# A two-layer hybrid encoder step: other layouts and another order for six small pieces of work

## The reference, cut to what matters

```
h = RMSNorm(x);  proj = h @ w_in        # columns go to four groups A, B, C, D of 256 channels
A: depthwise conv + RG-LRU scan         # lru_x, lru_g
B: latent attention: q from q_lat, k and v from 128-wide latents,
   new ones and 512 cached ones (past_ckv @ mla_wkv_b)
C: retention, 4 heads of 64             # r_q, r_k, r_v, r_g
D: mLSTM, 4 heads of 64                 # m_q, m_k, m_v, m_o, m_if
   dm = bh[t] - bh[s] + ig[s] (masked);  m_t = max(bh + m, max_s dm)
   sc = (q k^T) * exp(dm - m_t);  num = sc v + exp(bh + m - m_t) * (q C^T)
   state C <- gl * C + sum_s ws v k
x += concat(A, B, C, D, normed per head and gated) @ w_out
x += (silu(h2 @ w_g) * (h2 @ w_u)) @ w_down,   h2 = RMSNorm(x)
```

## Time and profile before

| | |
|---|---|
| median of three runs | 970.5 us (969.1 to 970.56) |
| the profiled execution | 969.53 us, of which the span of instructions is 967.7 us |
| TensorE busy | 951.0 us of the span, 98% |
| VectorE, ScalarE, GpSimd busy | 507.3, 200.7, 398.8 us |
| granted TensorE clock | 1.00 of full |
| HBM | 115 GB/s over the span |

### The profile page before, as it was taken

The page is one execution under the profiler, slowest core; times in us unless marked ns, Lnnn a source line. Parts: engine busy times, 40 slices in busy tenths (PEclk is TensorE's granted clock), DMA queues, the critical chain, the costliest instruction groups (busy, mean ns, idle before and its releaser), DMA issues. The chain is left out here.

```text
span 967.7 us, 15109 instructions
## 1 busy us (share of the span) xinstructions
PE 951.0 (98%) x5875; PEld 842.9 (87%) x5875; DVE 507.3 (52%) x1013; ACT 200.7 (21%) x440; POOL 398.8 (41%) x386
## 2 busy tenths in 40 slices
PE   7999999999999999999999999999999999999998
PEld 5777887877999999999967678777779999999998
DVE  5464546764756656512353545568465665654321
ACT  3113234533000100100021142344320110001001
POOL 8000110034866666676301003001268666666770
PEclk9999999999999999999999999999999999999999
DMA  9932211217655544343533311121175554434421
GB/s 250 267 114 87 90 48 45 70 24 181 162 137 147 151 132 132 121 152 120 142 105 100 108 63 50 44 88 50 13 205 142 150 144 132 131 124 139 142 95 37
DMA packets 159044, 112.14 MB, mean 116 GB/s; under 512 B 10103, under 2 KB 156957, under 8 KB 158845
## 3 DMA queue, kind: packets, MB, share of 16 engines
q1 hardware_dynamic: 154388, 104.50, 37.5%
q0 software_dynamic: 3952, 5.92, 2.3%
q10 hardware_dynamic: 632, 0.75, 0.3%
HBM read 108.89 MB, written 2.27 MB: 115 GB/s over the span
## 5 line engine op out<-in xcount | busy, mean ns | idle before, releaser
L729 PE MATMUL ps<-hT,ring 128*128 128x320 f32 x576 | 160.9, 435 | 0.1
L729 PEld LDWEIGHTS ps<-hT,ring 128*128 128x128 f32 x576 | 107.6, 190 | 45.8 <-DVE hT L1510 2.0
L600 POOL TENSOR_TENSOR work<-ring 128x512 f32<-128x512 f32 (+1 forms) x66 | 82.5, 1250 | 150.9 <-issue 116.0
L1077 PE MATMUL ps<-mixT,ring 128*128 128x160 f32 x672 | 105.0, 299 | 0.0
L1077 PE MATMUL ps<-hT,ring 128*128 128x160 f32 x672 | 98.9, 300 | 1.4 <-DVE hT L1965 1.3
L1077 PE MATMUL ps<-hT,work 128*128 128x160 f32 x672 | 98.6, 299 | 0.0
L1077 PEld LDWEIGHTS ps<-hT,ring 128*128 128x128 f32 x672 | 93.8, 190 | 2.5 <-DVE hT L1965 2.1
L1077 PEld LDWEIGHTS ps<-mixT,ring 128*128 128x128 f32 x672 | 95.9, 190 | 0.0
L1077 PEld LDWEIGHTS ps<-hT,work 128*128 128x128 f32 x672 | 93.6, 190 | 0.3
L601 POOL TENSOR_TENSOR ring<-ring 128x512 f32<-128x512 f32 (+1 forms) x66 | 83.2, 1261 | 5.2
L603 POOL TENSOR_TENSOR work<-ring,work 128x512 f32<-128x512 f32 (+1 forms) x66 | 83.2, 1261 | 5.2
(11 more groups left out here) (380 smaller groups left out, 1461.1 us busy)
## 6 DMA issues: line engine op xcount, KB each, us to landing
ring<-in_w_gu SPq DMA_DIRECT2D x88, 512.0 KB, 5.2
ring<-in_w_in SPq DMA_DIRECT2D x44, 512.0 KB, 4.8
ring<-in_w_down SPq DMA_DIRECT2D x32, 512.0 KB, 4.4
ring<-in_w_out SPq DMA_DIRECT2D x16, 512.0 KB, 4.1
ring<-in_w_down SPq DMA_DIRECT2D x16, 384.0 KB, 3.7
cst<-in_consts POOLq DMA_DIRECT2D x1, 1664.0 KB, 12.6
ring<-in_w_in SPq DMA_DIRECT2D x2, 640.0 KB, 6.7
wqb<-in_mla_wq_b POOLq DMA_DIRECT2D x2, 384.0 KB, 7.6
```

The source lines that it names most:

```text
L600: step(tt(s3, a11, a21, ALU.subtract))
L729: ins = mm(bank(use, 0, T, m), w[:, k, c:c + m], hT[:, k, 0:T], start=(k == 0), stop=(k == KT - 1))
L1077: ins = mm(bank(use, at * HT, HT), left, right(k), start=(opens and k == 0 and at == 0), stop=(closes and k == n - 1), skip_group_check=True)
```

## The change

- **Values by channel.** `mv` and `rv` are made by `feature` (two tiles of 8 products), copied by ScalarE to the scratch tile `wt` (`value_raw`), turned by three transposes each (`value_tiles`) and copied to `vaug` in two copies instead of three. `wt` gets a cleared pad for it.
- **Decays per token.** The decay of a query is made once for the 320 tokens (one product), and VectorE reads it in three parts instead of two.
- **Between D's score products.** The projection of C now stands ahead of `d_scores(h+1)`; ahead of the last `head_out` stand the key transposes of B's head 0 and half of `rv0`. On VectorE scores times decay h comes ahead of mask h+1, and the rows of B's keys come after that.
- **Smaller sums.** VectorE adds the two tiles of squared query latents, and `qms` is 3 products; `gx` is one product of 4 columns with a small diagonal matrix that VectorE makes, and two of 64.
- **Start of layer 0.** The norm sum is eight products on the squares themselves, three of them between the two halves of the input transposes; GpSimd's pair additions are gone. The 16 rows of `norm_mix` are loaded and turned alone, the other rows after `ql1`, and so are the cached latents with their four products.
- **Cached latents of layer 1** are turned inside layer 0's last down product, copied to `pastT` in the tile `ybm`. Two key tiles are handled ahead of `ql0` and two ahead of `ql1`.
- **GpSimd's mix 1** waits for `h_sums` 4 too.

```diff
-    d("ql0", "ql1", "kvr", "mo0", "mo1", "mig", "mfg", "mv0", "mv1", "mv2")
-    u += [("cnT", (4,)), ("qms", (5,)), ("qt0", (6,)), ("qt1", (7,)), ("qt2", (2,))]
+    d("ql0", "ql1", "kvr", "mo0", "mo1", "mig", "mfg", "mv0", "mv1")
+    u += [("cnT", (4,)), ("qms", (5,))]
+    d("mvt0", "mvt1")
+    u += [("qt0", (6,)), ("qt1", (7,)), ("qt2", (2,))]
...
-    fill = [("rv1", "rv2"), ("rqs0", "lx0", "rqs1"), ("rks0", "lx1", "rks1"), ("rg0",)]
+    fill = [("rv1",), ("rqs0", "lx0", "rqs1", "rvt0", "rvt1"), ("rks0", "lx1", "rks1"), ("rg0",)]
...
-                if i == 2:
+                if i == 1:
                     need(pool, "h_sums", l, 4)
...
-                    for n in range(3):
-                        pool.wait_ge(sem("squared"), 2 * n + 2)
-                        step(nc.gpsimd.tensor_tensor(hT[:, 2 * n, 0:T], hT[:, 2 * n, 0:T], hT[:, 2 * n + 1, 0:T], ALU.add),
-                             "sq_pairs")
...
+            turn_x(range(0, KT // 2))
+            claim(pe, "ms1", 0)
+            first_sum(range(0, 3))
+            turn_x(range(KT // 2, KT))
+            fill(first_sum(range(3, KT)), "ms1")
...
+            def value_tiles(which, l, p):
+
+                u = f"{which}t{p}"
+                claim(pe, u, l)
+                need(pe, "v_raw", l, 4, (0 if which == "mv" else 2) + p + 1)
+                if which == "rv":
+                    need(pe, "wt_pad", l, 1)
+                for t in range(NT):
+                    ins = nc.tensor.transpose(bank(u, t * P, P), wt[:, p, t * P:(t + 1) * P], ident)
+                fill(ins, u)
...
                 if l == 0:
+                    pe.wait_ge(sem("rows_loaded"), 16 * len(ROWLOADS))
+                    pe.wait_ge(sem("x_turned"), KT)
+                    nc.tensor.transpose(ps[:, 7, 0:NROWS], rows[:, :], ident[0:NROWS, 0:NROWS]).then_inc(
+                        sem("rows_turned"), 1)
+                    past_latents(0)
+                    pe.wait_ge(sem("cols_ready"), 2)
+                    need(pe, "past_T", l, 1)
+                    latents_out(PAST_TILES)
...
-                for t in range(NT):
-                    tokens(f"mv{t}", l, "mv", 0, G, t)
+                for p in range(2):
+                    feature(f"mv{p}", l, "mv", p * P, P)
...
-                    for p in range(2):
-                        ins = mm(bank("qms", t, 1), qls[:, p, t * P:(t + 1) * P], C("ones")[:, 0:1],
-                                 start=(p == 0), stop=(p == 1))
+                    ins = mm(bank("qms", t, 1), qls[:, 0, t * P:(t + 1) * P], C("ones")[:, 0:1], start=True, stop=True)
...
-                for h in range(H):
-                    mm(bank("gx", h, 1), C("headrow", H)[:, h * P:(h + 1) * P], r3[:, DEC - 1:DEC], start=True, stop=True)
+                mm(bank("gx", 0, H), C("ones", H), r3[:, DEC:DEC + H], start=True, stop=True)
...
-                    mm(bank(u, 0, 256), sel, r2[:, 0:256], start=True, stop=True)
-                    mm(bank(u, 256, 128), sel, r2[:, 128:256], start=True, stop=True)
-                    fill(mm(bank(u, 448, 64), sel, r2[:, 256:320], start=True, stop=True), u)
+                    fill(mm(bank(u, 0, T), sel, r2[:, :], start=True, stop=True), u)
...
                     if h + 1 < H:
-                        d_scores(h + 1)
                         u, name, p = (("rq1", "rq", 1), ("rk0", "rk", 0), ("rk1", "rk", 1))[h]
                         feature(u, l, name, p * P, P)
+                        d_scores(h + 1)
+                    else:
+                        turn_keys(0, "k")
+                        value_part(0, range(0, KT // 2))
...
+                        for p in range(2):
+                            value_tiles("rv", l, p)
...
+                        if l + 1 < DEPTH and q == NQ - 1 and r == 1:
+                            past_latents(l + 1)
...
-                    for a, n in SCORE_PARTS:
-                        step(v.tensor_tensor(dmx[:, a:a + n], bank(f"dd{h}", a, n), C("negmask")[:, a:a + n], ALU.add),
+                    for a, q0, n in ((0, 0, 256), (256, 128, 128), (448, 256, 64)):
+                        step(v.tensor_tensor(dmx[:, a:a + n], bank(f"dd{h}", q0, n), C("negmask")[:, a:a + n], ALU.add),
...
                     need(dve, "decay_d", l, H, h + 1)
-                    if h + 1 < H:
-                        decay_arg(h + 1)
                     wait_filled(dve, f"ds{h}", l)
...
                     step(tails(h, dh[:, h % 2, :], HD + 1), "w_d")
+                    if h + 1 < H:
+                        decay_arg(h + 1)
+                    if h == 0:
+                        key_rows()
                     if h > 0:
                         d_out(h - 1)
```

More of the change, by code:

```diff
@@ L191 @@
 NCH = len(CHUNKS)
-LAST_USE = {"kvr": "kvr", "ql": "ql1", "mo": "mo1", "mv": "mv2", "mq": "mq1", "mk": "mk1", "rq": "rq1",
-            "rk": "rk1", "rg": "rg1", "rv": "rv2", "lx": "lx1", "lg": "lg1"}
+LAST_USE = {"kvr": "kvr", "ql": "ql1", "mo": "mo1", "mv": "mv1", "mq": "mq1", "mk": "mk1", "rq": "rq1",
+            "rk": "rk1", "rg": "rg1", "rv": "rv1", "lx": "lx1", "lg": "lg1"}
 LAST_USE.update({f"o{i}": f"o{2 * i + 1}" for i in range(4)})
@@ L701, in _, with turn_x, first_sum @@
             pe.wait_ge(sem("x_cleared"), 1)
[L702 to L707 removed]
+            def turn_x(ks):
+                pe.wait_ge(sem(f"x_loaded{ks[0] // (KT // 2)}"), 48)
+                for k in ks:
+                    for t in range(NT):
+                        ins = nc.tensor.transpose(ps[:, k, t * P:(t + 1) * P], xtm[:, t, k * P:(k + 1) * P], ident)
+                    ins.then_inc(sem("pre_filled"), 1)
+            def first_sum(ks):
+                for k in ks:
+                    need(pe, "squared", 0, 2 * KT, k + 1)
+                    ins = mm(bank("ms1", 0, T), C("ones"), hT[:, k, 0:T], start=(k == 0), stop=(k == KT - 1),
+                             skip_group_check=True)
+                return ins
+            turn_x(range(0, KT // 2))
[3 more added lines that the diff above has]
+            fill(first_sum(range(3, KT)), "ms1")
             def norm_sum(use, l):
                 claim(pe, use, l)
[L710 to L711 removed]
+                for n, k in enumerate((0, KT - 2, KT - 1)):
                     if k >= KT - 2:
                         need(pe, "squared", l, 2 * KT, k + 1)
[L714 to L715 removed]
                     else:
@@ L937, in between @@
                     if h == 0:
-                        for t in range(1, NT):
-                            tokens(f"rv{t}", l, "rv", 0, G, t)
+                        feature("rv1", l, "rv", P, P)
                     elif h == 1:
@@ L996, in weigh_values @@
                     fill(mm(bank(u, 128, 64), pT[0:64, 384:512], vb[0:64, 2, h, :], start=False, stop=True), u)
-                turn_keys(0)
-                tokens("rv0", l, "rv", 0, G, 0)
+                turn_keys(0, "q")
+                value_part(0, range(KT // 2, KT))
+                need(pe, "vb_ready", l, KTILES)
                 chunk_scores(0)
@@ L1305, in _ @@
                 rsqrt_(l, small[:, 16:16 + NT], bank("qms", 0, NT), QR, name="qlat_rstd", use="qms")
+                for p in range(2):
+                    value_copy("mv", "d", p)
                 need(act, "q_copied", l, 1)
@@ L1411, in _ @@
                 conv_input(0)
+                for p in range(2):
+                    value_copy("rv", "c", p)
                 probs_copy(1)
```

223 lines of the change are left out of this document (125 added, 98 removed).

## The result

The changed kernel takes 963.23 us (median of 4 runs, 962.46 to 963.5) beside 970.04 us for the kernel before: a ratio of 0.993, with a 95% interval of 0.9912 to 0.9947. The forecast was 958.5 with a range of 955.0 to 962.0. The direction was right; the time is 1.2 us above the range, 4.7 above the forecast. The one execution that was profiled in experiment 4 for the kernel with the small tables held ran at a granted clock of 0.65 throughout and took 1414 us, so of its trace only one DMA time is used.

A forecast was written before the change was run, and what follows sets the result against it. TensorE, busy 951.0 of 967.7 us, was taken to bound the kernel. The terms sum to -12.0 us against the profiled 969.53, giving 957.5; the runs' median lies 1.0 higher: 958.5 us, range 955.0 to 962.0.

The forecast's parts named there:

- the term for layer 0's start: Layer 0 up to `kvr`: new order starts `kvr` near 31.9 instead of 29.75, +2.2 us, bounds +0.5 and +3.5.
- The clock: Rival: TensorE's clock falls to 1.2 GHz after new holes at layer 0's start; 971.5 us, chance 0.03.
- Values by channel, -3.5: Two value projections in two layers: feature tiles plus transposes at 0.115 us replace token tiles, saving 3.5 us.
- The wait at `rvt0`, +1.0: Transposes of `rvt0` wait about 0.5 us per layer for ScalarE's copies of `lx0`: +1.0 us, bounds 0 and 1 a layer.
- Smaller sums, -3.0: `qms` and `gx` each lose 3 products per layer, saving 1.4 and 1.6 us over both layers.
- Decays per token, -3.7: D's eight heads: one 320-column product of 0.55 us replaces three parts of 1.01 us, saving 3.7 us, at least 3.
- D's order, -1.8: Around D's heads: reordering removes TensorE's two waits for the weighted values of head 0, saving 1.8 us.
- Start of layer 1, -1.6: Layer 1's waits for the latents' copy and at `kvr` go, saving 1.6 us, bounds 1.0 and 2.1.
- Mix 1, -1.6: Holding GpSimd's mix 1 speeds VectorE's 640-column products and removes layer 1's TensorE wait: -1.6 us, bounds 0 and -2.3.
- rivals of D's order: D's new order gives back what it saves, 1 us a layer and 0.5 more at `rvt0`: 961.5 us, chance 0.12.
- the late mix: Rival: held-back mix 1 ends 0.8 us after TensorE wants it, in both layers: 961.7 us, chance 0.08.
- the start pay as meant: Rival: layer 0's projections begin at 17.6 instead of 20.70 and the 2.2 us loss vanishes: 956 us, chance 0.15.

The follow-up runs named there:

- experiment 4: Changed kernel with GpSimd's small tables and the 1664 KB load behind them held: 956.9 us; with the 1664 KB load alone held: 963.72 us.
- experiment 1: Changed kernel with GpSimd's constant and table loads held until six tiles of x are squared: 957.49 us, ratio 0.9873.
- experiment 2: Changed kernel with 28 extra unused products keeping TensorE busy while the ql weights are awaited: 961.22 us, ratio 0.9906.
- experiment 3: Kernel before the change, with GpSimd's 680 KB load of constants issued ahead of its three pair additions: 970.67 us, ratio 1.0003.

## Why the prediction missed, step by step

**The failed step** is the term for layer 0's start: "+2.2 us, bounds +0.5 ... and +3.5 (if the `ql` weights, of which the trace only shows that they were there by 20.70, come after 17.6; GpSimd now issues its loads earlier and competes)". It measured +8.3, and what the prediction gave as its sign of being wrong ("if the start loses over 4 us") came. The products and copies in it were right as a sum: with the loads held, `kvr` starts at 31.47 where 31.9 was worked out. The step named the mechanism and gave it 1.3 us without working it out. Two rows were missing: when `ql` lands (15.9 us in the kernel before, only 1.1 to 1.7 ahead of the new need at 17.0 to 17.6), and how many loads stand behind the pair additions in GpSimd's queue (18). With the DMA engines at a busy share of 1.04 to 1.15 in every window of 2 us from 6 to 18 us of the kernel before, a margin of 1.5 us against 18 loads moved 5.6 us earlier is no bound of 1.3; several microseconds were the honest upper end, as experiments 1 and 4 show.

**The clock** was a rival with 13 us for a clock that stayed low through 48 records. It came through 6 us of them and cost 2.1 (experiment 2). I had leaned on a hole of 3.08 us that was followed by records at full pace; the new wait was 6.7, but a hole of 2.91 us in nearly the same place was enough in experiment 3, so that row was no safe ground.

**The rest of the sum** (-14.2, measured -14.0 to -14.4) came out partly by luck: the decays gave 1.5 us less than their term, and values, layer 1's start, D's order and mix 1 together about as much more. The smaller sums and layer 1's start were not undone in a kernel of their own; their figures are differences between two traces.

**Values by channel, -3.5:** right in kind, a little more in size. Transposes stand 0.115 us apart (six from 64.62 to 65.31), D's projection gives 1.14 a layer for 0.87: two feature tiles take 8.72 us (8.82 in the term) and three token tiles 10.47 (10.38).

```profile
64.03 0.73 PE L876 MATMUL ps<-cst,arena 128*128 128x1 f32 x6
64.62 0.85 PE L751 MATMUL ps<-cst,work 128*128 128x128 f32 x6
65.31 1.13 PE L883 MATMUL ps<-wqb,arena 128*128 128x384 f32 x3
```

By the figure of the Trainium skill ("TensorE: Matmul & The Clock Gate", Part 4: PE-mode transpose), which is for bf16, these six would have taken 1.65 us (an estimate, 6 x 0.275); the trace has 0.69 and the undone kernels are slower, not faster. The measurement decides.

**The wait at `rvt0`, +1.0:** there, in both layers.

```profile
146.53 0.70 PE L972 MATMUL ps<-work,cst 128*128 128x320 f32 x2
147.54 0.90 PE L751 MATMUL ps<-cst,work 128*128 128x128 f32 x6 [0.30 <-ACTq L435]
```

1.01 us stand between these starts, about 0.47 of them more than two such records need.

**Smaller sums, -3.0:** `mq` to `rq0` gave 1.3 for 1.6, and `kvr` to `mq`, where `qms` lies beside D's values, 3.6 for 3.1.

**Decays per token, -3.7:** mechanism right, size off: 2.2 by the spacing, 1.9 by the trace of the undone kernel, both below the "as little as -3" that was allowed for. The step "One product of 320 columns is 2 x 0.27" took the pace of 128 partitions for 4, though the old parts' own pace stood in the same rows.

**D's order, -1.8:** right, 2.1; no wait is shown at `head_out` 3, so its 4.4 us did about fit into 4.5 (half of `rv0` takes 2.28 us to the next start there, 2.15 with the decays in three parts, so 0.1 may be lost). **Start of layer 1, -1.6:** 1.8; the waits at L808 and `kvr` are gone, and the norm sum now waits a little for squares:

```profile
489.12 1.95 PE L820 MATMUL ps<-wkvb,work 128*128 128x512 f32 x4
490.91 2.12 PE L729 MATMUL ps<-hT,cst 128*128 128x320 f32 x6
492.87 1.88 PE L820 MATMUL ps<-wkvb,work 128*128 128x512 f32 x4
494.89 9.13 PE L740 MATMUL ps<-hT,ring 128*128 128x320 f32 x32
```

**Mix 1, -1.6:** 2.1. VectorE's four products take 3.82 us, not 7.02 and less than the 5.2 expected, and no product waits for GpSimd:

```profile
706.49 3.82 DVE L2031 TENSOR_TENSOR hT<-work,rstd 128x640 f32<-128x640 f32 x4 [3.25 <-ACT rstd L1259]
```

The rivals of D's order and of the late mix did not come; nor did the start pay as meant; with the loads held and the latents in the hole it costs nothing (`kvr` at 29.80, 29.75 before) and the kernel takes 954.99.

## What to carry to other kernels

When work is taken off an engine that also issues loads, write down every load that stood behind it, the landing time of what they will share the DMA engines with, and the margin to its first use; a start-up load with 1.5 us of margin is not hidden. When a wait can't be removed, put independent work of the same engine into it: early loads cost 5.7 us in one order and 2.2 in another. And undo parts with the cover left as it was: the value tiles cost 4.5 us in halves and 10.7 in one piece, through a wait that the new place itself made and the clock behind it.

## What the runs showed of the hardware that I had not expected

- Sixteen small loads of about 0.6 MB on GpSimd's queue, among them rows repeated over the partitions and scattered rows, put the end of a 1 MB load on SyncE's queue off by about 5 us (landing 18.2 us after issue, 12.8 with them held), behind a 680 KB load that cost it 0.8 alone. While they are under way the DMA engines are busy at a share of 1.00 and move 138 GB/s, with them held 301 GB/s at 1.15.
- The granted clock fell to 0.50 for about 6 us after waits of 6.7 us and, once, of 1.72 us, and for 2 to 4 us after waits of 2.91 and 3.35. It stayed at 1.00 after one of 1.72 us in the other layer of the same execution, after 1.70 us (experiment 1), 1.6 (D's old order) and 3.08 (the kernel before). The length of a wait alone doesn't tell. A fall cost 2.1 us at `ql` and 3.35 in the first kernel with token tiles.
- A 320-column product over 4 partitions holds TensorE 0.365 us a record (102.30 to 103.03, two records), one over 128 partitions 0.27 (4.41 us for 16 records).
